# Key and value tiles of two heads a load, and a bias table written by units of two heads

## What is computed

```python
q, k, v, gate = split(rms_norm(x) @ w_in)           # 2048, 256, 256, 2048 columns
q = rms_norm(q.reshape(.., 4, 8, 64), q_gain)       # 32 query heads, 8 to a key head
k = rms_norm(k.reshape(.., 4, 64), k_gain)          # 4 key heads
dist = qi + L - kj                                  # a block of 128 queries, 256 keys
bias = rel_table[t5_bucket(max(dist, 0))]           # for each of 32 heads, [128, 256]
s = q @ k.T * 64 ** -0.5 + bias                     # outside the band: -inf
m = max(max(s), sink)
p = exp(s - m) / (sum(exp(s - m)) + exp(sink - m))
x = x + ((p @ v) * silu(gate)) @ w_out
```

## Time and profile before

| | us |
|---|---|
| median of three runs | 1877.64 |
| lowest and highest | 1875.6, 1878.66 |
| the profiled execution | 1878.74 |
| its span | 1877.0 |

### The profile page before, as it was taken

The page is one execution under the profiler, slowest core; times in us unless marked ns, Lnnn a source line. Parts: engine busy times, 40 slices in busy tenths (PEclk is TensorE's granted clock), DMA queues, the critical chain, the costliest instruction groups (busy, mean ns, idle before and its releaser), DMA issues.

```text
span 1877.0 us, 28406 instructions
## 1 busy us (share of the span) xinstructions
PE 1833.1 (98%) x9917; PEld 1546.1 (82%) x9917; DVE 936.7 (50%) x2320; ACT 868.4 (46%) x2026; POOL 36.9 (2%) x65
## 2 busy tenths in 40 slices
PE   7899999999998999999999999999999999979999
PEld 5688888888876888898888988889888888958887
DVE  5356565565655333554545646454564645544221
ACT  4356666565655322443534445353544534453221
POOL 1000000000001000000000000000000000000000
PEclk9999999999998999999999999999999999979999
DMA  7922222222215444332222213222222222214442
GB/s 188 224 73 83 80 81 74 80 81 82 80 34 142 129 138 139 102 87 79 71 80 80 78 57 91 78 71 77 80 73 73 81 78 70 67 33 129 135 134 84
DMA packets 297107, 173.47 MB, mean 92 GB/s; under 512 B 22880, under 2 KB 285616, under 8 KB 297024
## 3 DMA queue, kind: packets, MB, share of 16 engines
q1 hardware_dynamic: 290256, 151.28, 28.6%
q0 software_dynamic: 5696, 20.25, 4.5%
q10 hardware_dynamic: 1088, 1.08, 0.3%
HBM read 156.86 MB, written 14.66 MB: 91 GB/s over the span
## 4 chain that ended last, share of the span: by engine, by line
PE 94%; DMA 2%; DVE 1%; ACT 1%; SPq 0%; issue 0%; ACTq 0%; DVEq 0%
PE G L480 78%; DMA raw<-in_swa_w_in 2%; PE G L601 1%; PE O L841 1%; PE S L812 1%; PE S L766 1%; PE O L601 1%; PE O L784 1%; PE G L588 1%; PE S L578 1%; PE S L577 1%; PE T L588 1%; PE G L728 1%; PE G L563 1%; PE S L830 1%; PE S L827 0%
## 5 line engine op out<-in xcount | busy, mean ns | idle before, releaser
L480 PE MATMUL G<-xh,wh 128*128 128x512 f32 (+1 forms) x2624 | 891.6, 371 | 8.0 <-DVE xl L1562 4.9
L480 PE MATMUL G<-xl,wh 128*128 128x512 f32 (+1 forms) x2624 | 844.7, 354 | 0.0
L480 PE MATMUL G<-xh,wl 128*128 128x512 f32 (+1 forms) x2624 | 841.3, 352 | 0.0
L480 PEld LDWEIGHTS G<-xh,wh 128*128 128x128 f32 x2624 | 465.0, 189 | 91.4 <-issue 22.5
L480 PEld LDWEIGHTS G<-xh,wl 128*128 128x128 f32 x2624 | 461.8, 189 | 70.2
L480 PEld LDWEIGHTS G<-xl,wh 128*128 128x128 f32 x2624 | 461.8, 189 | 63.3 <-issue 4.8
L1377 DVE TENSOR_TENSOR wl<-raw,wh 128x512 fp32r<-128x512 f32 x528 | 354.2, 688 | 305.5 <-ACT wh L918 301.6
L918 ACT ACTIVATE wh<-raw 128x512 fp32r<-128x512 f32 x528 | 315.5, 620 | 127.5 <-PE G L480 102.0
L1252 ACT ACTIVATE att<-att,st 128x144 f32<-128x144 f32 (+3 forms) x64 | 36.9, 577 | 128.9 <-DVE wmeta L1771 70.3
L1015 ACT ACTIVATE p<-S,rq 128x256 f32<-128x256 f32 (+1 forms) x128 | 50.2, 444 | 47.8 <-PE S L578 46.3
L1478 DVE TENSOR_TENSOR st<-st 128x1 f32<-128x1 f32 x128 | 20.3, 159 | 87.7 <-ACT st L1027 87.7
(11 more groups left out here) (240 smaller groups left out, 1731.8 us busy)
## 6 DMA issues: line engine op xcount, KB each, us to landing
raw<-in_w_in SPq DMA_DIRECT2D x112, 512.0 KB, 4.0
raw<-in_swa_w_in SPq DMA_DIRECT2D x72, 512.0 KB, 4.0
raw<-in_swa_w_out SPq DMA_DIRECT2D x32, 512.0 KB, 5.1
raw<-in_w_out SPq DMA_DIRECT2D x32, 512.0 KB, 4.7
raw<-in_w_in POOLq DMA_DIRECT2D x8, 1024.0 KB, 8.1
rel_rows<-relb POOLq DMA_DIRECT2D x1, 6128.0 KB, 38.4
mixed<-in_x SPq DMA_DIRECT2D x4, 1024.0 KB, 8.7
bias<-rel_rows POOLq DMA_DIRECT2D x16, 256.0 KB, 3.3
```

The costliest lines, as they stand in the source:

```text
L480: mm = pe.matmul(d, w[:, slot, k, :], v[:, k, a:b], start=(k == 0 and n == 0), stop=(k == KC - 1 and n == 2))
```

## The change

- Tiles 0 to 3 hold other columns. Tile c = 0, 1 has the keys of heads 2c and 2c + 1, tile 2, 3 the values of two heads. A tile's 128 columns are one run, so a tile is one transfer of 1 MB with rows of 512 bytes where there were two of 256 bytes a row.
- The chain is done per kind: statistics and norm for the two key tiles (`key_stat`, `key_finish`, on all 128 partitions), with four copies to `kh2` and four subtractions for `kl2` each; transposes for the two value tiles alone (`value_transpose`, at point 5 of tiles 3 and 4), with two copies to `v2` each.
- The table is written unit by unit: `bias_write(i, g)` writes the rows of two heads. Before each `bias_rows`, POOL waits for that unit's write, and issues the next unit's write right behind it.
- `relb` has memory of its own now (in place of `rel_end`), and ACT's first eviction waits for rel_ok in place of rel_out.

```diff
-        relb = sb("relb", [HEADS, REL_COLS], scope=rel)
         rel.close()
         p1 = sb("p1", [P, 4, 2 * P], scope=one)
-        rel_end = sb("rel_end", [P, 160], scope=one)
+        relb = sb("relb", [HEADS, REL_COLS], scope=one)
...
             def kv_weights(g):
                 after(sp, w_lo, 4 * (g - 2) + 4)
-                for half, col in enumerate((SWA_K, SWA_V)):
-                    sp.dma_start(raw[:, g % 2, :, HD * half:HD * half + HD],
-                                 w1_v[:, :, col + HD * g:col + HD * g + HD]).then_inc(raw_in[g % 2], 16)
+                sp.dma_start(raw[:, g % 2, :, :], w1_v[:, :, SWA_K + P * g:SWA_K + P * g + P]).then_inc(raw_in[g % 2], 16)
...
             pool.wait_ge(rel_ok, 1)
-            pool.dma_start(bass.AP(tensor=rel_rows.tensor, offset=0,
-                                   ap=[[P * REL_PITCH, HEADS], [REL_PITCH + 1, P], [1, REL_COLS]]),
-                           relb[:, :].rearrange("h (a n) -> h a n", a=1).broadcast_to([HEADS, P, REL_COLS])).then_inc(rel_out, 16)
-            pool.wait_ge(rel_out, 16)
-            bias_rows(0, 0)
+
+            def bias_write(i, g):
+
+                h = 8 * g + 2 * i
+                pool.dma_start(bass.AP(tensor=rel_rows.tensor, offset=h * P * REL_PITCH,
+                                       ap=[[P * REL_PITCH, 2], [REL_PITCH + 1, P], [1, REL_COLS]]),
+                               relb[h:h + 2, :].rearrange("h (a n) -> h a n", a=1)
+                               .broadcast_to([2, P, REL_COLS])).then_inc(rel_out, 16)
+
+            def bias_of(i, g):
+                pool.wait_ge(rel_out, 16 * (4 * i + g + 1))
+                bias_rows(i, g)
+                if (i, g) != (UNITS - 1, KV - 1):
+                    bias_write(*((i, g + 1) if g + 1 < KV else (i + 1, 0)))
+
+            bias_write(0, 0)
+            bias_of(0, 0)
             pool.wait_ge(sink_ok, 1)
...
-            def kv_transpose(g):
-                if g:
-                    pe.wait_ge(kv_v, g)
+            def key_stat(c):
+                pe.wait_ge(kv_raw, c + 1)
+                pe.matmul(G[:, c, :], head_ones, chain_sq[:, 0:TOK], start=True, stop=True).then_inc(kv_stat, 1)
+
+            def value_transpose(g):
+                pe.wait_ge(kv_ev, g + 1)
+                if g == KV // 2:
+                    pe.wait_ge(rel_ok, 1)
                 else:
-                    pe.wait_ge(rel_ok, 1)
+                    pe.wait_ge(kv_v, 2)
                 for t in range(NB):
                     mm = pe.transpose(T[:, P * t:P * t + P], chain_raw[:, P * t:P * t + P], ident)
                 mm.then_inc(kv_t, 1)
...
-                    if g and p == 5:
-                        kv_stat_of(g - 1)
-                    if g and p == 6:
-                        kv_transpose(g - 1)
+                    if 0 < g <= KV // 2 and p == 5:
+                        key_stat(g - 1)
+                    if g > KV // 2 and p == 5:
+                        value_transpose(g - 1)
...
-            def kv_split(g):
-                act.wait_ge(kv_n, g + 1)
-                for half in range(2):
-                    A(kh2[HD * half:HD * half + HD, g, :], qn[0:HD, :], ACT.Copy).then_inc(kv_hi, 1)
+            def key_split(c):
+                act.wait_ge(kv_n, c + 1)
+                for a in range(2):
+                    for half in (a, 1 - a):
+                        A(kh2[HD * half:HD * half + HD, 2 * c + a, :], qn[HD * a:HD * a + HD, :], ACT.Copy).then_inc(kv_hi, 1)
...
+            def value_rows(v):
+                dve.wait_ge(kv_t, v + 1)
+                for a in range(2):
+                    V.tensor_copy(v2[:, 2 * v + a, :, :, :], T[:, :].rearrange("p (t a n) -> p t a n", t=NB, a=2)[:, :, a:a + 1, :]
+                                  .broadcast_to([P, NB, 2, HD])).then_inc(kv_v, 1)
```

More of the change, by code:

```diff
@@ L448, in _ @@
                 if g:
-                    bias_rows(0, g)
+                    bias_of(0, g)
                 sinks_of(0, g)
@@ L452, in _ @@
                 for g in range(KV):
-                    bias_rows(i, g)
+                    bias_of(i, g)
                     sinks_of(i, g)
@@ L893, in kv_loaded @@
             def kv_loaded(g):
-                return (raw_in[g % 2], 32 * (g // 2 + 1), "whole") if g < KV else unit_loaded(0, 0)
+                return (raw_in[g % 2], 16 * (g // 2 + 1), "whole") if g < KV else unit_loaded(0, 0)
             def unit_loaded(u, half):
@@ L1009, in swa_evict @@
                 if isinstance(u, int) and u == 0:
-                    act.wait_ge(rel_out, 16)
+                    act.wait_ge(rel_ok, 1)
                 after(act, a_t, 4 * u + j - 1)
@@ L1427, in kv_evict @@
                 dve.wait_ge(rs1_ok, 1)
-                after(dve, kv_t, g)
-                after(dve, kv_n, g)
+                if 0 < g <= KV // 2:
+                    dve.wait_ge(kv_n, g)
+                elif g:
+                    dve.wait_ge(kv_t, g - KV // 2)
                 V.tensor_tensor(chain_raw[:, 0:TOK], G[:, g, :], rs1[:, :], ALU.mult).then_inc(kv_ev, 1)
-            def kv_finish(g):
-                dve.wait_ge(kv_rs, g + 1)
-                if g:
-                    dve.wait_ge(kv_lo, 2 * g)
-                V.scalar_tensor_tensor(out=qn[0:HD, :], in0=chain_raw[0:HD, 0:TOK], scalar=gains[0:HD, 1:2],
-                                       in1=chain_rs[0:HD, 0:TOK], op0=ALU.mult, op1=ALU.mult).then_inc(kv_n, 1)
-                dve.wait_ge(kv_t, g + 1)
-                V.tensor_copy(v2[:, g, :, :, :], T[:, :].rearrange("p (t a n) -> p t a n", t=NB, a=2)[:, :, 1:2, :]
-                              .broadcast_to([P, NB, 2, HD])).then_inc(kv_v, 1)
@@ L1443, in kv_split, with key_finish @@
-            def kv_split(g):
-                for half in range(2):
-                    dve.wait_ge(kv_hi, 2 * g + 1 + half)
-                    V.tensor_tensor(kl2[HD * half:HD * half + HD, g, :], qn[0:HD, :], kh2[0:HD, g, :].bitcast(F32),
-                                    ALU.subtract).then_inc(kv_lo, 1)
+            def key_finish(c):
+                dve.wait_ge(kv_rs, c + 1)
+                if c:
+                    dve.wait_ge(kv_lo, 4 * c)
+                V.scalar_tensor_tensor(out=qn[:, :], in0=chain_raw[:, 0:TOK], scalar=gains[:, 1:2],
+                                       in1=chain_rs[:, 0:TOK], op0=ALU.mult, op1=ALU.mult).then_inc(kv_n, 1)
@@ new lines, in key_split @@
+            def key_split(c):
+                for a in range(2):
+                    g, lo, hi = 2 * c + a, HD * a, HD * a + HD
+                    for half in range(2):
+                        dve.wait_ge(kv_hi, 2 * g + 1 + half)
+                        V.tensor_tensor(kl2[HD * half:HD * half + HD, g, :], qn[lo:hi, :], kh2[lo:hi, g, :].bitcast(F32),
+                                        ALU.subtract).then_inc(kv_lo, 1)
+            def value_rows(v):
+                dve.wait_ge(kv_t, v + 1)
+                for a in range(2):
+                    V.tensor_copy(v2[:, 2 * v + a, :, :, :], T[:, :].rearrange("p (t a n) -> p t a n", t=NB, a=2)[:, :, a:a + 1, :]
+                                  .broadcast_to([P, NB, 2, HD])).then_inc(kv_v, 1)
@@ L1453, in _ @@
                     if m == 7:
-                        kv_finish(g - 1)
-                        kv_split(g - 1)
+                        if g <= KV // 2:
+                            key_finish(g - 1)
+                            key_split(g - 1)
+                        else:
+                            value_rows(0)
                     if m % 2 == 0:
```

45 lines of the change are left out of this document (17 added, 28 removed).

## The result

| | us | lowest, highest | runs |
|---|---|---|---|
| kernel before | 1877.05 | 1875.6, 1878.66 | 4 |
| changed kernel | 1864.89 | 1863.87, 1866.53 | 4 |
| its profiled execution | 1864.97 (span 1863.3) | | |

The ratio is 0.9931, with a 95% interval of 0.9918 to 0.9945: 12.2 us gained, where 14.5 were forecast. The forecast was 1863.1.

What follows compares the result with a forecast made beforehand. The prediction took the tensor engine as the bound and summed 9.22 + 2.52 + 2.8 = 14.54 us, from the median of 1877.64 to a forecast of 1863.1 us. The range was 1859.0 to 1869.0.

Steps and rivals of the forecast that it cites:

- The bound: Whole kernel: the tensor engine bounds it; an edit is worth the work, idle time or slow clock it removes there.
- Part 1: Tile 4: writing the table by units removes the late weight load's stall, two holes and the slow clock after each, 9.22 us.
- Part 2: Key and value tiles: two statistics and two sets of transposes fewer on the tensor engine, 2 x 1.26 = 2.52 us.
- The longer key chain: Tiles 1 and 2: more copies and subtractions make the next squares some 1.4 us later; cost 0, at most 1.3.
- Part 3: Start: loads of 512-byte rows bring x's second quarter sooner, 2.8 us taken between bounds of 1.9 and 3.5.
- The lower bound: Start: 1 MB keeps the DMA engines busy 5.46 us in 256-byte rows, 3.53 in 512-byte rows; 1.9 us gained.
- The upper choice: Start: 2.8 us taken, as the second half load took 4.4 us where 512-byte rows need 1.8.
- Rival 1: Start: the clock holds over the shorter hole, 2.1 us more gained, 1861.0 us; chance 0.18.
- Rival 2: Unit writes run on few, same DMA engines; some 4.5 us of stall by tiles 5 and 6, 1867.6 us; chance 0.12.
- Rival 3: Units: writes from 28 us on set the unit's period; with 32 us writes 1916 us, slower than before; chance 0.04.
- Rival 4: Tile 4: its stall has another cause, or first writes still delay the weights; 2.52 + 2.8 left, 1872.3 us; chance 0.06.
- The added POOL work: Units: POOL issues one more DMA a unit, estimated at 0.71 us each, hidden by its waiting; cost taken as 0.

Runs made afterwards that it cites:

- write_only: The kernel before with the bias table written unit by unit alone, tiles 0 to 3 and their loads as before: 1868.69 us, ratio 0.9948.
- before_late: The kernel before with POOL's twelve small start loads issued only after x's last quarter has landed: 1876.22 us, ratio 0.999.
- small_late: The changed kernel with POOL's twelve small start loads issued only after x's last quarter has landed: 1860.91 us, ratio 0.9908.
- quarter_first: small_late with the first quarter of tile 0's weights loaded ahead of x's second quarter, the rest behind it: 1860.65 us, ratio 0.9908.
- tiles_only: The changed kernel with the one large write of the bias table put back: 1872.38 us, ratio 0.9966.
- sinks_late: The changed kernel with only the sinks' load issued after x's last quarter has landed: 1865.09 us, ratio 0.9933.
- rows256_late: small_late with each key and value load split into two of 256-byte rows: 1861.66 us, ratio 0.9916.

## Why the prediction was right, and where not

The time fell inside the range and 1.8 us from the forecast. Two of three terms measured as worked out, and the third did not: it was the smaller part of the sum, so the forecast could stand without it.

1. *The bound* held: the tensor engine, and gains counted as what leaves its stream.
2. *Part 1, 9.22 us*: 9.26 us in the trace of `write_only`, 9.0 in its time. The step that compared tile 4 with tile 3 was right. The reason given for "the whole of it goes" was half wrong: 1.8 us for a write "if the writes spread over the DMA engines". They don't. The sixteen writes landed 18.2 to 20.7 us after their issues, at two engines' worth of work, and the tile weights beside them land after 11.4 us in the middle and 18.8 at most, not 3.6. From issue to landing, for `raw` between 40 and 90 us:

```profile
DMA to landing us min/median/max: 5.6/11.4/18.8
```

   The gain stood because of the other reason, the long way from issue to use: tile 4's first load is issued at 45.1 and the tensor engine comes to the tile at 73.67. The nearest reader is sooner, though. The two loads of tile 4 landed at 63.9 and 65.3, and ACT's split reads them from 65.43 on, some 1.5 us after the first. The list of waits from 44 to 100 us has no wait of ACT's split for `raw` left. POOL waits for its write twice, 35.7 us in all, and nobody waits for POOL:

```profile
POOL bias L426 <- DMA rel_rows<-relb: 35.7, 2, 18.1
```

   The rule of the Trainium skill (DMA: Bandwidth & Descriptors, Why a DMA increments its semaphore by 16 and not by 1) gave 16 engines for 32 heads and 2 for two heads. The shares of POOL's queue, 97.3% and 11.8%, agree, and the 92.3% of the one-head writes agree with the next dimension, 128, taking over. The rule says nothing of the rate, and there it was not enough.
3. *Part 2, 2.52 us*: 2.55, from `write_only` to the changed kernel. The longer key chain cost nothing, as argued: the squares of the second key tile are at 56.30 and the statistics want them at 58.45.
4. *Part 3, 2.8 us*: 0.55 in the profile, which is inside the spread of one start. This is the step that failed, and its 2.25 us account for the difference between the sum (14.54) and the 12.34 of the profile; tile 5 starts at 85.25, not near 83.0. The bounds, 1.9 to 3.5, were both above what the kernels that differ in the rows alone show, for two reasons. The first is the price of the rows themselves: even with the small loads away they are worth 1.2 us of the start, not 2.8. The lower bound took its 1.9 from the engines' busy time in a quiet stretch; the rates of the start itself, 290 and 218 GB/s, give 1.2. The second is that x waited for something else as well, POOL's small loads, beside which the row size shows nothing. The upper choice read the second half load's 11.7 us as the price of its rows, when the same small loads stood in it; with them away (`before_late`) it is 9.3. A row of before showed it, in the queues of the start: from 9 to 10 us POOL's 108 packets with 0.01 MB took 64.2% of the engines' time and SP's 173 took 19.5%.

```profile
q0 software_dynamic: 108, 0.01, 64.2%
q1 hardware_dynamic: 173, 0.04, 19.5%
```

5. *Rival 1 (the clock holds)*: no. The hole was 5.00 us, and two rounds of transposes and products behind it took 4.05 us (16.76 to 20.81) where they took 4.24. Even behind holes of 2.75 and 2.16 us, in `small_late` and `quarter_first`, it came.
6. *Rival 2 (few engines)*: its first condition came out near to the number, 18.9 us for 18.5 and loads of 11.4 in the middle for 11.5; its result, a stall in tile 5 or 6, did not come. Its chance of 0.12 was put on few engines and the same ones each time. Only the first is shown; that the engines changed is inferred from the missing stall, as the trace doesn't name them. *Rival 3* would have needed 28 us a write; the 16 writes landed 18.2 to 20.7 us after their issues. *Rival 4* is shut out by `write_only`.
7. *The added POOL work*, put at 0: at most 0.65 us. The first unit's statistics and the last's are 449.65 us apart, and were 449.00. `tiles_only`, without the unit writes, has 449.46 and `write_only`, with them, 449.50, so the writes are not shown to be the cause.

## What to carry to other kernels

Look at the queues' shares of the DMA engines in every stretch that a term rests on, and at the start above all: 0.12 MB of small loads asked for beside the first tiles cost this kernel 4 us, and a wait of one line in front of them gives it back (1860.9; no form with more edits was faster by more than the noise). Before a small term is read from one profile, compare profiles of kernels that have the same code there: here they lay 2.3 us apart. A transfer cut into pieces need not be cheap to be harmless: landing after 19 us and not 4, the unit writes hide, because the weight loads beside them are issued far enough ahead, if with little to spare. Parts of a change that remove the same hole need not add up when tried alone.

## What the runs showed of the hardware

- A write from SBUF that reads one row at a time (one head, 128 shifted copies) had nearly all 16 DMA engines taken, 92.3%, at 26 GB/s. Two rows took 11.8%, the time of two engines: 24 GB/s. 32 rows: 203 GB/s (2.03 MB in 10 us).
- A load that reads one row of 128 bytes for 128 partitions (the sinks) went as sixteen packets of 1 KB that took 0.8 to 1.4 us each in the changed kernel; a 2 KB packet of x took 0.084.
- POOL's packets of 4 and 16 bytes took 0.5% of the engines' time in a microsecond in which SP's queue moved 0.20 MB, where it moved 0.41 without them (`sinks_late`, `small_late`, 5 to 6 us).
- With the small loads away, key and value weights in 512-byte rows went in at 290 GB/s, in 256-byte rows at 218 (8 to 9 us, `small_late` and `rows256_late`).
- The column of the granted clock can miss a slow stretch: in the changed kernel it says 1.00 from 17 to 20 us, where products are 0.43 us apart. There the spacing is the better witness.
